# Other start addresses for the expert matmuls' operands: split weights on multiples of 128 bytes, tokens and activations 64 bytes past one

## The chip, the cores and the metric

One core of one Trainium2 chip runs the whole program. The metric is the device time in microseconds of one execution; the kernel before was run three times.

## The reference, cut to what matters

A two-layer decoder trunk for 256 tokens of width 1024, float32. Layer 0 is a recurrent mixer and a dense SwiGLU, layer 1 attention and a mixture of eight experts, of which each token takes two:

```python
h = h + rglru_mixer(rmsnorm(h), ...)
h = h + swiglu(rmsnorm(h), ffn_w_gate, ffn_w_up, ffn_w_down)       # width 3584
h = h + swa_sink_mixer(rmsnorm(h), ...)
for e in range(8):                                                   # top 2 of 8
    out += comb[..., e:e+1] * (silu(h @ w_gate[e]) * (h @ w_up[e])) @ w_down[e]
h = h + out
return rmsnorm(h)
```

The experts' weights are 8 x 3 x 1024 x 3584 floats, 352 MB, and their matmuls are most of the work.

## The kernel before, in words

**Precision.** Float32 matmuls in the experts and the dense layers are replaced by three passes in the type fp32r: each operand is split into a high part (a cast) and a low part (the operand less its high part), and the passes are high by high, low tokens by high weights, high tokens by low weights (`PASSES`, L1437).

**Weights.** SyncE loads pieces of 1 MB (128 partitions x 2048 floats) into `ring`, 14 slots. ScalarE copies a slot into `w_hi` (L663, for the experts) and VectorE writes slot less `w_hi` into `w_lo` (L1252). Both have three parts (`PARTS`), used in turn. `hi_done`, `lo_done` and `parts_used` are the counters between the three engines; a slot is loaded again when `lo_done` says that it has been split (`load`, L416 to L431). The dense layers use the same parts, through `split_dense` (L478, L841), 56 pieces in all (`SPLITS`), and the experts go on from there.

**Experts.** For one expert up to 96 tokens (`CAP`) are gathered into `xg_hi` and `xg_lo`, eight chunks of 128 x 96. The width 3584 is done in 14 steps of 256 (`NCH`). In a step, `gate_up` (L1842 to L1852) does gate and up: the stationary operand is a chunk of `xg`, the moving one 256 columns of a weight piece, 3 x 8 matmuls each. `turn_h` (L1854) transposes the product, `stage_ht` casts it to `ht_hi` and `ht_lo`, and `down` (L1861 to L1875) takes these as stationary operand and moves 512 columns of the down piece, 12 matmuls. So there are 8 x 14 = 112 steps with 48 matmuls at L1850 and 12 at L1872. `cross` overlaps an expert's end with the next one's start; `scatter` (L1819) adds an expert's output back, with `y_hi`, `y_lo` stationary and `gt_r` moving.

**Dense layers.** In `ffn_gate_up` (L1540) it is the other way round: weights are stationary (128 columns), activations `u_hi`, `u_lo` move (256 columns). `project_back` (L1486) and `project_out` (L1705) do the same with `z` and the heads. `project` (L1602) of attention has activations stationary (128 columns) and weights moving (256).

**Addresses.** Tensors lie one after the other. `ring` starts on a multiple of 128 bytes, and `gap`, 16 floats, lies behind it, so `w_hi` and `w_lo` start 64 bytes past a multiple of 128. `gap2`, 16 floats, brings what follows (`h`, `hn`, `work`, ..., `xg_hi`, `xg_lo`, `ht_hi`, `ht_lo`, `cst`) back onto multiples. The dense activations and `y_hi`, `gt_r`, `y_lo` are views laid over this memory by a first list of tensors ("below"), on multiples of 128 too. Below, "+64" is 64 bytes past a multiple of 128, and "0" is on one.

| matmul | stationary | moving |
|---|---|---|
| experts L1850, L1872 | xg, ht: 0 | w_hi, w_lo: +64 |
| dense L1540, L1486, L1705 | w_hi, w_lo: +64 | u, z, heads: 0 |
| attention L1602 | u: 0 | w_hi, w_lo: +64 |
| scatter L1819 | y: 0 | gt_r: 0 |

**Order.** Every engine's order is written out by hand. ScalarE enters the experts by `first_lead` (L704): first split, staging of xg, further splits, after `keep_tokens` (L648). TensorE's last use of a dense part is the end of `project_out(3)` (called at L1775), before the router's results.

Of the kernel before, what the change touches and what calls it, by code (L numbers as in the profile page):

```python
# [19 lines left out]
P = 128  # L20
D = 1024
KC = D // P
T = 256
# [15 lines left out]
SLOTS = 14  # L39
DENSE = 7  # L40
SLOT = 2048
PARTS = 3
PIECES = 3 * NCH

MAX_OVER = (TOPK * T - 1) // CAP
# [4 lines left out]

LRU_LOADS, FFN_LOADS, ATT_LOADS = 13, PIECES, 10
GATES_AT = 4
# [4 lines left out]
ATT_SPLITS = LRU_SPLITS + FFN_LOADS  # L57
SPLITS = ATT_SPLITS + ATT_LOADS
FIRST_SPLIT = LRU_LOADS - LRU_SPLITS
BELOW_Y = 16 + 2 * PARTS * SLOT + 16 + KC * T + D  # L60
BELOW_GT = 2048 + 4 * CAP
ORDER_MOE = [(DENSE_LOADS + n) % DENSE for n in range(DENSE)] + list(range(DENSE, SLOTS))

# [3 lines left out]
F32 = mybir.dt.float32  # L67
F32R = mybir.dt.float32r
# [51 lines left out]
def trunk(nc, x, positions, params, lru_gates, lru_w_in, lru_w_out, attn_w_qkv, attn_b_qkv, attn_sinks, attn_w_o,  # L120
          ffn_w_gate, ffn_w_up, ffn_w_down, moe_w_gate, moe_w_up, moe_w_down, norm_final, consts, out):
    with ExitStack() as ctx:
        def sb(name, shape, dt=F32):
            return ctx.enter_context(nc.sbuf_tensor(name, shape, dt))

        def sem(name):
            return ctx.enter_context(nc.semaphore(name))

        with (nc.sbuf_tensor("below", [P, 7 * SLOT], F32), nc.sbuf_tensor("z_lo", [P, KC, T], F32R) as z_lo,
              nc.sbuf_tensor("below_aa", [P, SLOT], F32), nc.sbuf_tensor("z_hi", [P, KC, T], F32R) as z_hi,  # L130
              nc.sbuf_tensor("below_u", [P, SLOT], F32), nc.sbuf_tensor("u_hi", [P, KC, T], F32R) as u_hi,
              nc.sbuf_tensor("u_lo", [P, KC, T], F32R) as u_lo, nc.sbuf_tensor("f_hi", [P, 2, 2, T], F32R) as f_hi,
              nc.sbuf_tensor("f_lo", [P, 2, 2, T], F32R) as f_lo, nc.sbuf_tensor("below_y", [P, BELOW_Y], F32),
              nc.sbuf_tensor("y_hi", [P, D], F32R) as y_hi, nc.sbuf_tensor("below_gt", [P, BELOW_GT], F32),
              nc.sbuf_tensor("gt_r", [P, T], F32R) as gt_r, nc.sbuf_tensor("y_lo", [P, D], F32R) as y_lo):
            pass
        ring = sb("ring", [P, SLOTS, SLOT])
        gap = sb("gap", [P, 16])
        w_hi, w_lo = sb("w_hi", [P, PARTS, SLOT], F32R), sb("w_lo", [P, PARTS, SLOT], F32R)
        gap2 = sb("gap2", [P, 16])  # L140
        h = sb("h", [P, KC, T])
        hn = sb("hn", [P, KC, T])
        work = sb("work", [P, 2048])
# [3 lines left out]
        zero_mem = sb("zero_mem", [1, 512], BF16)  # L147
        mask_mem = sb("mask_mem", [P, 4 * P], BF16)

        xg_hi, xg_lo = sb("xg_hi", [P, KC, CAP], F32R), sb("xg_lo", [P, KC, CAP], F32R)  # L150
        ht_hi, ht_lo = sb("ht_hi", [P, 2, 2, CAP], F32R), sb("ht_lo", [P, 2, 2, CAP], F32R)
        cst = sb("cst", [P, NCONST])
        par = sb("par", [P, NPAR])
        small = sb("small", [P, 256])
# [131 lines left out]
        hi_done, lo_done, parts_used = sem("hi_done"), sem("lo_done"), sem("parts_used")  # L286
# [19 lines left out]
        def load_of(j):  # L306
            return FIRST_SPLIT + j

        def slot_at(j):
            return slot_of[load_of(j)]  # L310
# [61 lines left out]
        def _(sp):  # L372
# [43 lines left out]
            def load(i, e, at, places, first=False):  # L416

                for n, (what, c, ahead) in enumerate(places, at):
# [5 lines left out]
                    else:  # L424
                        sp.wait_ge(lo_done, PIECES * i + (SPLITS - SLOTS + n + 1))
                    if what == "down":
# [28 lines left out]
        def _(act):  # L455
# [17 lines left out]
            def split_dense(j):  # L473

                act.wait_ge(loaded[slot_at(j)], arrive[load_of(j)])
                if j >= PARTS:
                    act.wait_ge(parts_used, j - PARTS + 1)
                nc.scalar.copy(w_hi[:, j % PARTS], ring[:, slot_at(j)]).then_inc(hi_done, 1)  # L478

# [87 lines left out]

            for j in range(PARTS, FFN_LOADS + 1):
                if j < FFN_LOADS:
                    split_dense(LRU_SPLITS + j)  # L570
                what, c = FFN_PIECES[j - PARTS] if j < FFN_LOADS else ("up", NCH - 1)
# [86 lines left out]
            def split(i, n):  # L658

                s = ORDER_MOE[n % SLOTS]  # L660
                act.wait_ge(loaded[s], 48 * i + (moe_base[s] + 16 * (n // SLOTS + 1)))
                act.wait_ge(parts_used, PIECES * i + (SPLITS - PARTS + n + 1))
                nc.scalar.copy(w_hi[:, (SPLITS + n) % PARTS], ring[:, s]).then_inc(hi_done, 1)  # L663

            def weights_back(i):
                act.wait_ge(g_turned, i + 1)
# [7 lines left out]
            def stage_xg(i):  # L674
                for g in range(2):
                    act.wait_ge(gathered, 2 * i + (g + 1))
                    nc.scalar.copy(xg_hi[:, 4 * g:4 * g + 4], ps[:, 4 + g, 0:4 * CAP].rearrange("p (c n) -> p c n", c=4)).then_inc(xg_hi_ready, 1)

            def silu(i, c, up_at):
                act.wait_ge(parts_used, PIECES * i + (SPLITS + up_at + 1))  # L680
                nc.scalar.activation(h_tok[:, c % 2], ps[0:CAP, c % 2, 0:CHF], ACT.Silu).then_inc(m_silu, 1)
# [5 lines left out]
            def stage_y(i, down_at):  # L687
                act.wait_ge(parts_used, PIECES * i + (SPLITS + down_at + 1))
                nc.scalar.copy(y_tok[:, 0:512], ps[0:CAP, 2, :]).then_inc(y_staged, 1)

            def split_y(i, down_at):
                act.wait_ge(parts_used, PIECES * i + (SPLITS + down_at + 1))
                act.wait_ge(slot_w_ready, i)
                for m in range(2):
                    nc.scalar.activation(y_hi[0:CAP, 512 * m:512 * m + 512], ps[0:CAP, 2 + m, :], ACT.Copy, scale=slot_w[0:CAP]).then_inc(y_hi_ready, 1)

            def lead(i):
                split(i, 0)
                split(i, 1)
                split(i, 2)  # L700
                split(i, 3)
                silu(i, 0, 1)

            def first_lead():  # L704
                split(0, 0)
                stage_xg(0)
                split(0, 1)
                split(0, 2)
                act.wait_ge(gap_ready, 1)
                nc.scalar.activation(gate[:, 0:2], gate[:, 0:2], ACT.Exp).then_inc(gap_exp, 1)  # L710
                split(0, 3)
                silu(0, 0, 1)
# [28 lines left out]
            def finish(i, first=False):  # L741
# [11 lines left out]
                stage_y(i, END_AT + 1)  # L753

            first_lead()
            body(0, None)
            for i in range(E - 1):
# [27 lines left out]
        def _(dve):  # L785
# [8 lines left out]
            V = nc.vector  # L794
# [7 lines left out]
            a, n = ROWS["lam"]  # L802
# [3 lines left out]
            a, n = ROWS["b_a"]  # L806
# [182 lines left out]
            for j in range(PARTS, FFN_LOADS + 1):  # L989
                what, c = FFN_PIECES[j - PARTS] if j < FFN_LOADS else ("up", NCH - 1)  # L990
# [257 lines left out]
            def split(i, n):  # L1248

                part = (SPLITS + n) % PARTS  # L1250
                dve.wait_ge(hi_done, PIECES * i + (SPLITS + n + 1))
                V.tensor_tensor(w_lo[:, part], ring[:, ORDER_MOE[n % SLOTS]], w_hi[:, part].bitcast(F32),  # L1252
                                ALU.subtract).then_inc(lo_done, 1)

            def stage_xg(i):
# [36 lines left out]
            def lead(i):  # L1292
                split(i, 0)
                split(i, 1)
                split(i, 2)
                split(i, 3)
                gate_times_up(i, 0)
# [133 lines left out]
        def _(pe):  # L1431
# [391 lines left out]
            def parts(i, n):  # L1823

                pe.wait_ge(hi_done, PIECES * i + (SPLITS + n + 1))
                return w_hi[:, (SPLITS + n) % PARTS], w_lo[:, (SPLITS + n) % PARTS]

            def low_part(i, n):

# [175 lines left out]
```

## Time and profile before

| | |
|---|---|
| median of 3 runs | 1464.48 us (1464.02 to 1464.84) |
| span of the profiled execution | 1463.9 us |
| TensorE matmul busy | 1434.9 us |
| VectorE busy | 1167.5 us |
| ScalarE busy | 925.6 us |
| read from HBM | 423.44 MB |

The profiled execution is one run by itself; its span stands 0.6 us under the median of the runs. TensorE's matmuls overlap: a row of the timeline gives the start of the first of a run of matmuls and the time to the end of the last, so the pace is read from the starts of rows that follow each other.

### The profile page before, as it was taken

To read this page: it belongs to the slowest core of one execution; us is meant where nothing else is said; L and a number is where in the kernel's file an instruction comes from. 1 tells how busy PE (TensorE), PEld (TensorE's weight loads), DVE (VectorE), ACT (ScalarE), POOL (GpSimd) and SP (SyncE) were. 2 spreads that over 40 slices of the span, in tenths; PEclk is the share of its full clock that TensorE was granted. 3 is DMA by queue.
4 is the path that set the end of the run, shared out by engine and by line. 5 is a ranking of instruction groups with operands and counts; after the bars stand their busy time and mean duration, and the time that the engine had idled before them with its cause. 6 is when DMAs were issued, how large, how long until landed. Compare 5 with 4: busy or idle time off the path is not lost.

```text
span 1463.9 us, 25480 instructions
## 1 busy us (share of the span) xinstructions
PE 1434.9 (98%) x10712; PEld 1312.7 (90%) x10712; DVE 1167.5 (80%) x1101; ACT 925.6 (63%) x918; POOL 42.5 (3%) x62
## 2 busy tenths in 40 slices
PE   7999999999999999999999999999999999999996
PEld 6899999998889889999999888999999898999994
DVE  6676556568637998998988998899798889989895
ACT  3845434444516777776776767676676767767675
POOL 2030000003020000000000000000000000000000
PEclk9999999999998999999999999999999999999998
DMA  8466555553219998999999999899999989999931
GB/s 332 144 227 227 189 189 199 199 184 136 72 49 417 368 382 336 366 363 339 357 348 368 332 378 360 335 357 353 351 349 361 367 342 354 357 350 360 355 146 45
DMA packets 60001, 426.14 MB, mean 291 GB/s; under 512 B 7025, under 2 KB 7153, under 8 KB 8689
## 3 DMA queue, kind: packets, MB, share of 16 engines
q1 hardware_dynamic: 58752, 422.60, 77.5%
q10 hardware_dynamic: 1136, 1.91, 0.4%
q8 instruction: 86, 1.41, 0.4%
q14 instruction: 27, 0.21, 0.0%
HBM read 423.44 MB, written 1.05 MB: 290 GB/s over the span
## 4 chain that ended last, share of the span: by engine, by line
PE 96%; ACT 1%; DVE 1%; POOL 1%; issue 1%; DMA 0%; ACTq 0%; SPq 0%; POOLq 0%; DVEq 0%
PE ps L1850 42%; PE ps L1872 21%; PE ps L1540 10%; PE ps L1563 5%; PE ps L1454 3%; PE ps L1838 2%; PE ps L1602 2%; PE ps L1486 2%; PE ps L1705 1%; PE ps L1857 1%; PE ps L1819 1%; PE ps L1649 1%; PE ps L1469 1%; POOL hn L1412 1%; PE ps L1677 0%
## 5 line engine op out<-in xcount | busy, mean ns | idle before, releaser
L1252 DVE TENSOR_TENSOR w_lo<-ring,w_hi 128x2048 fp32r<-128x2048 f32 x336 | 766.6, 2290 | 98.7 <-ACT w_hi L663 96.7
L663 ACT CAST w_hi<-ring 128x2048 fp32r<-128x2048 f32 x336 | 641.0, 1911 | 163.4 <-PE ps L1850 163.4
L1850 PE MATMUL ps<-w_hi,xg_hi 128*96 128x256 f32 x1792 | 248.6, 281 | 1.2 <-DVE xg_lo L1258 1.2
L1850 PE MATMUL ps<-w_hi,xg_lo 128*96 128x256 f32 x1792 | 241.8, 277 | 0.0
L1850 PE MATMUL ps<-w_lo,xg_hi 128*96 128x256 f32 x1792 | 241.6, 277 | 0.0
L1850 PEld LDWEIGHTS ps<-w_hi,xg_lo 128*96 128x96 f32 x1792 | 216.0, 161 | 0.0
L1850 PEld LDWEIGHTS ps<-w_lo,xg_hi 128*96 128x96 f32 x1792 | 215.7, 161 | 0.0
L1850 PEld LDWEIGHTS ps<-w_hi,xg_hi 128*96 128x96 f32 x1792 | 214.2, 162 | 1.3 <-DVE xg_lo L1258 1.3
L841 DVE TENSOR_TENSOR w_lo<-ring,w_hi 128x2048 fp32r<-128x2048 f32 x56 | 130.1, 2325 | 74.1 <-ACT w_hi L478 74.0
L478 ACT CAST w_hi<-ring 128x2048 fp32r<-128x2048 f32 x56 | 106.7, 1907 | 98.3 <-PE ps L1540 87.4
L1872 PE MATMUL ps<-w_lo,ht_hi 128*96 128x512 f32 x448 | 123.5, 397 | 0.2 <-DVE w_lo L1252 0.2
L1872 PE MATMUL ps<-w_hi,ht_hi 128*96 128x512 f32 x448 | 122.3, 395 | 0.3 <-ACT w_hi L663 0.3
L1872 PE MATMUL ps<-w_hi,ht_lo 128*96 128x512 f32 x448 | 122.2, 394 | 0.0
L1872 PEld LDWEIGHTS ps<-w_lo,ht_hi 128*96 128x96 f32 x448 | 72.1, 161 | 33.1 <-DVE w_lo L1252 0.7
L1872 PEld LDWEIGHTS ps<-w_hi,ht_lo 128*96 128x96 f32 x448 | 72.3, 161 | 31.7
L685 ACT CAST ht_hi<-ps 128x192 fp32r<-128x192 f32 x112 | 35.7, 319 | 91.5 <-PE ps L1857 91.2
L1872 PEld LDWEIGHTS ps<-w_hi,ht_hi 128*96 128x96 f32 x448 | 67.1, 162 | 15.9 <-ACT w_hi L663 0.5
L1540 PE MATMUL ps<-u_hi,w_hi 128*128 128x256 f32 x448 | 55.8, 277 | 0.0
L1540 PE MATMUL ps<-u_lo,w_hi 128*128 128x256 f32 x448 | 55.5, 276 | 0.0
L1540 PE MATMUL ps<-u_hi,w_lo 128*128 128x256 f32 x448 | 55.5, 276 | 0.0
L1540 PEld LDWEIGHTS ps<-u_hi,w_hi 128*128 128x128 f32 x448 | 53.0, 188 | 0.5 <-issue 0.4
L1268 DVE TENSOR_TENSOR ht_lo<-ps,ht_hi 128x192 fp32r<-128x192 f32 x112 | 38.6, 345 | 18.2 <-ACT ht_hi L685 18.2
(286 smaller groups left out, 1376.4 us busy)
## 6 DMA issues: line engine op xcount, KB each, us to landing
ring<-in_moe_w_gate SPq DMA_DIRECT2D x112, 1024.0 KB, 6.8
ring<-in_moe_w_up SPq DMA_DIRECT2D x112, 1024.0 KB, 6.7
ring<-in_moe_w_down SPq DMA_DIRECT2D x112, 1024.0 KB, 6.8
ring<-in_ffn_w_gate SPq DMA_DIRECT2D x14, 1024.0 KB, 4.8
ring<-in_ffn_w_up SPq DMA_DIRECT2D x14, 1024.0 KB, 4.8
ring<-in_ffn_w_down SPq DMA_DIRECT2D x14, 1024.0 KB, 4.9
ring<-in_lru_w_in SPq DMA_DIRECT2D x7, 1024.0 KB, 12.4
ring<-in_attn_w_qkv SPq DMA_DIRECT2D x6, 1024.0 KB, 4.8
```

The lines of the kernel that those rows point to most:

```text
L478: nc.scalar.copy(w_hi[:, j % PARTS], ring[:, slot_at(j)]).then_inc(hi_done, 1)
L663: nc.scalar.copy(w_hi[:, (SPLITS + n) % PARTS], ring[:, s]).then_inc(hi_done, 1)
L685: nc.scalar.copy(ht_hi[:, c % 2], ps[:, 6 + c % 2, 0:2 * CAP].rearrange("p (f n) -> p f n", f=2)).then_inc(ht_hi_ready, 1)
L841: V.tensor_tensor(w_lo[:, j % PARTS], ring[:, slot_at(j)], w_hi[:, j % PARTS].bitcast(F32), ALU.subtract).then_inc(lo_done, 1)
L1252: V.tensor_tensor(w_lo[:, part], ring[:, ORDER_MOE[n % SLOTS]], w_hi[:, part].bitcast(F32), ALU.subtract).then_inc(lo_done, 1)
L1268: V.tensor_tensor(ht_lo[:, c % 2], ps[:, 6 + c % 2, 0:2 * CAP].rearrange("p (f n) -> p f n", f=2), ht_hi[:, c % 2].bitcast(F32), ALU.subtr ...
L1454: mm = nc.tensor.matmul(ps[:, p % 4, f * T:(f + 1) * T], col[:, k, f * P:(f + 1) * P], u_raw[:, k], start=(k == 0), stop=(k == KC - 1))
L1486: mm = nc.tensor.matmul(ps[:, p, f * T:(f + 1) * T], w[b][:, k, f * P:(f + 1) * P], zs[a][:, k], start=False, stop=(k == KC - 1 and b == 1 ...
L1540: mm = nc.tensor.matmul(ps[:, 2 * (c % 2) + f, m * T:(m + 1) * T], w[b][:, k, f * P:(f + 1) * P], us[a][:, k], start=(j > 1 and k == 0 and ...
L1563: mm = nc.tensor.matmul(ps[:, 4 + d // 2, (d % 2) * T:(d % 2 + 1) * T], w[b][:, f, d * P:(d + 1) * P], fs[a][:, c % 2, f], start=False, st ...
L1850: mm = nc.tensor.matmul(ps[0:CAP, c % 2, m * CHF:(m + 1) * CHF], xs[a][:, k], w[b][:, k], start=(k == 0 and (a, b) == (0, 0)), stop=(k == ...
L1872: mm = nc.tensor.matmul(ps[0:CAP, 2 + g, :], hs[a][:, c % 2, f], w[b][:, f, g * 512:(g + 1) * 512], start=(c == 0 and f == 0 and (a, b) == ...
```

## The change

`w_hi` and `w_lo` each become a piece of memory with 16 floats (`SHIFT`) before and behind the three parts. The views `w_hi`, `w_lo`, used by the dense layers and attention, begin 16 floats into it and stay 64 bytes past a multiple of 128. A second pair of views, `e_hi` and `e_lo`, begins at its start, on a multiple of 128, and is what the experts' splits write and their matmuls read. The gaps move: one before `xg_hi` puts `xg` and `ht` 64 bytes past a multiple, one behind `ht_lo` brings the rest back. Since part k of the second views covers the end of part k - 1 of the first, ScalarE waits, before the experts' first split, until all 56 dense pieces have been used, where it waited for 54. The padding is counted in `BELOW_Y`.

```diff
+SHIFT = 16
-BELOW_Y = 16 + 2 * PARTS * SLOT + 16 + KC * T + D
+BELOW_Y = 2 * (SHIFT + PARTS * SLOT + SHIFT) + KC * T + D
...
         ring = sb("ring", [P, SLOTS, SLOT])
-        gap = sb("gap", [P, 16])
-        w_hi, w_lo = sb("w_hi", [P, PARTS, SLOT], F32R), sb("w_lo", [P, PARTS, SLOT], F32R)
-        gap2 = sb("gap2", [P, 16])
+        w_hi_mem = sb("w_hi", [P, SHIFT + PARTS * SLOT + SHIFT], F32R)
+        w_lo_mem = sb("w_lo", [P, SHIFT + PARTS * SLOT + SHIFT], F32R)
+        w_hi, w_lo = (a[:, SHIFT:SHIFT + PARTS * SLOT].rearrange("p (n c) -> p n c", n=PARTS) for a in (w_hi_mem, w_lo_mem))
+        e_hi, e_lo = (a[:, 0:PARTS * SLOT].rearrange("p (n c) -> p n c", n=PARTS) for a in (w_hi_mem, w_lo_mem))
...
+        gap = sb("gap", [P, SHIFT])
         xg_hi, xg_lo = sb("xg_hi", [P, KC, CAP], F32R), sb("xg_lo", [P, KC, CAP], F32R)
         ht_hi, ht_lo = sb("ht_hi", [P, 2, 2, CAP], F32R), sb("ht_lo", [P, 2, 2, CAP], F32R)
+        gap2 = sb("gap2", [P, SHIFT])
...
             def split(i, n):                       # ScalarE
...
-                nc.scalar.copy(w_hi[:, (SPLITS + n) % PARTS], ring[:, s]).then_inc(hi_done, 1)
+                nc.scalar.copy(e_hi[:, (SPLITS + n) % PARTS], ring[:, s]).then_inc(hi_done, 1)
...
             def first_lead():
+                act.wait_ge(parts_used, SPLITS)
                 split(0, 0)
...
-                V.tensor_tensor(w_lo[:, part], ring[:, ORDER_MOE[n % SLOTS]], w_hi[:, part].bitcast(F32),
+                V.tensor_tensor(e_lo[:, part], ring[:, ORDER_MOE[n % SLOTS]], e_hi[:, part].bitcast(F32),
                                 ALU.subtract).then_inc(lo_done, 1)
...
             def parts(i, n):                       # TensorE
                 pe.wait_ge(hi_done, PIECES * i + (SPLITS + n + 1))
-                return w_hi[:, (SPLITS + n) % PARTS], w_lo[:, (SPLITS + n) % PARTS]
+                return e_hi[:, (SPLITS + n) % PARTS], e_lo[:, (SPLITS + n) % PARTS]
```

## Rows read from the trace of the kernel before

**Rows 1.** The page's span, and its 40 slices: TensorE's clock, DMA share, rate.
```profile
span 1463.9 us, 25480 instructions
PE 1434.9 (98%) x10712; PEld 1312.7 (90%) x10712; DVE 1167.5 (80%) x1101; ACT 925.6 (63%) x918; POOL 42.5 (3%) x62
...
PEclk9999999999998999999999999999999999999998
DMA  8466555553219998999999999899999989999931
GB/s 332 144 227 227 189 189 199 199 184 136 72 49 417 368 382 336 366 363 339 357 348 368 332 378 360 335 357 353 351 349 361 367 342 354 357 350 360 355 146 45
```

**Rows 2.** The page's chain that ended last, shares of the span by line.
```profile
PE ps L1850 42%; PE ps L1872 21%; PE ps L1540 10%; PE ps L1563 5%; PE ps L1454 3%; PE ps L1838 2%; PE ps L1602 2%; PE ps L1486 2%; PE ps L1705 1%; PE ps L1857 1%; PE ps L1819 1%; PE ps L1649 1%; PE ps L1469 1%; POOL hn L1412 1%; PE ps L1677 0%
```

**Rows 3.** One expert: us, busy PE, PEld, DVE, ACT, POOL, clock, DMA share, GB/s.
```profile
577.00:702.00 125.00, 125.00 (x927) 112.75 (x927) 109.83 (x83) 89.26 (x76) 0.00 (x0) 1.00 0.95 354
```

**Rows 4.** Waits: who for whom, us in total, times, longest us.
```profile
ACT w_hi L663 <- PE ps L1850: 163.4, 204, 1.7
```

**Rows 5.** Timeline of TensorE, a quick step: start us, us, operation, count.
```profile
585.89 1.14 PE L1850 MATMUL ps<-w_hi,xg_hi 128*96 128x256 f32 x8
586.87 1.07 PE L1850 MATMUL ps<-w_hi,xg_lo 128*96 128x256 f32 x8
587.77 1.07 PE L1850 MATMUL ps<-w_lo,xg_hi 128*96 128x256 f32 x8
...
591.40 1.09 PE L1872 MATMUL ps<-w_hi,ht_hi 128*96 128x512 f32 x4
...
594.20 0.33 PE L1857 MATMUL ps<-cst,hn 96*128 96x96 f32 x2
```

**Rows 6.** Timeline of TensorE, a slow step.
```profile
613.29 1.10 PE L1850 MATMUL ps<-w_hi,xg_lo 128*96 128x256 f32 x8
614.23 1.10 PE L1850 MATMUL ps<-w_lo,xg_hi 128*96 128x256 f32 x8
...
617.97 1.09 PE L1872 MATMUL ps<-w_hi,ht_hi 128*96 128x512 f32 x4
...
620.76 0.33 PE L1857 MATMUL ps<-cst,hn 96*128 96x96 f32 x2
```

**Rows 7.** Timeline of TensorE in the dense feed-forward layer.
```profile
161.05 1.98 PE L1540 MATMUL ps<-u_lo,w_hi 128*128 128x256 f32 x16
...
164.68 1.52 PE L1540 MATMUL ps<-u_hi,w_hi 128*128 128x256 f32 x12
```

**Rows 8.** Timeline of TensorE: projections of attention, and a scatter.
```profile
331.27 2.04 PE L1602 MATMUL ps<-w_lo,u_hi 128*128 128x256 f32 x16
...
345.82 1.98 PE L1602 MATMUL ps<-w_lo,u_hi 128*128 128x256 f32 x16
...
435.16 2.05 PE L1705 MATMUL ps<-u_hi,w_lo 128*128 128x256 f32 x16
...
603.06 0.28 PE L1819 MATMUL ps<-gt_r,y_hi 96*128 96x256 f32 x1
...
603.65 0.28 PE L1819 MATMUL ps<-gt_r,y_lo 96*128 96x256 f32 x1
```

**Rows 9.** The page's groups: busy us, mean ns, idle before and releaser.
```profile
L1252 DVE TENSOR_TENSOR w_lo<-ring,w_hi 128x2048 fp32r<-128x2048 f32 x336 | 766.6, 2290 | 98.7 <-ACT w_hi L663 96.7
L663 ACT CAST w_hi<-ring 128x2048 fp32r<-128x2048 f32 x336 | 641.0, 1911 | 163.4 <-PE ps L1850 163.4
...
L1850 PE MATMUL ps<-w_hi,xg_lo 128*96 128x256 f32 x1792 | 241.8, 277 | 0.0
L1850 PE MATMUL ps<-w_lo,xg_hi 128*96 128x256 f32 x1792 | 241.6, 277 | 0.0
...
L1540 PE MATMUL ps<-u_hi,w_lo 128*128 128x256 f32 x448 | 55.5, 276 | 0.0
```

**Rows 10.** Timeline of ScalarE at the entry of the experts.
```profile
442.62 1.90 ACT L663 CAST w_hi<-ring 128x2048 fp32r<-128x2048 f32 x1
```

## The prediction

> **What bounds the kernel now.** I began with the page of the kernel before. TensorE is busy for 98% of the span at full granted clock, POOL hardly works, and the DMA engines are loaded in the second two thirds [rows 1]. The chain that ended last, by line, is TensorE's too: 42% of the span at L1850 (gate and up of the experts) and 21% at L1872 (down), so the two lines that the change touches hold 63% of what sets the end [rows 2]. The stretch of one expert says how much room the others have: in 125 us TensorE works for 125, VectorE for 109.83, ScalarE for 89.26, and DMA moves 354 GB/s [rows 3]. Of the waits, ScalarE's weight copies stand 163.4 us behind L1850 and show no wait for a load: data and splits are early, TensorE is late [rows 4]. So time can only be won or lost by how fast a matmul follows the one before it.
>
> That pace is not a row's mean duration, since matmuls overlap; it is the distance from start to start in the timeline. In a quick step of expert 1, eight 256-column matmuls start at 586.87 and the next eight at 587.77, and such a row is 1.07 us long [rows 5]. In a slow step of the same expert the rows are 1.10 us and 0.94 apart [rows 6]. So 113.4 ns a matmul in one and some 117 in the other: with 276 to 277 ns for the last of eight [rows 9], (1.07 - 0.276)/7 = 113.4 and (1.10 - 0.276)/7 = 117.7. Same code, same addresses, same clock. Over the whole program the 1792 matmuls of w_hi with xg_lo are busy 241.8 us, 224 rows of eight [rows 9]: 1.079 us a row, a third of the way from 1.07 to 1.10.
>
> **What the addresses have to do with it.** The change alters the address (modulo 128 bytes) of both operands of these two lines and no instruction count, so the question is which pairings the trace already shows. Before, the experts have moving +64, stationary 0. The dense feed-forward L1540 has the pairing that the change makes, stationary weights at +64 and moving activations at 0: two rows of 16 go from 161.05 to 164.68, 3.63/32 = 113.4 ns [rows 7], and over all 448 of one part 55.5 us in 28 rows is 1.98 us each [rows 9], as in [rows 7]: this pairing is at the quick pace throughout, although VectorE and ScalarE split there too. The attention projection L1602 has the pairing of before, with 128 columns: 2.04 us for 16 in one place and 1.98 in another [rows 8], slow and quick. Two rows speak against a simple rule: L1705, stationary +64 and moving 0, takes 2.05 for 16 [rows 8], so the new pairing can be slow too. And the scatter L1819, both at 0, takes (603.65 - 603.06)/5 = 118 ns [rows 8].
>
> The Trainium skill speaks against any effect: "SBUF — State Buffer" (Who interferes with whom) gives TensorE two independent read ports, for the moving operand and for LDWEIGHTS, and says that TensorE waits on nobody; its specifications count lines of 16 bytes, of which a shift of 64 is a whole number. By it the sum below would be zero. The trace has no run with one address alone changed; its two paces at one address [rows 5, 6] neither follow from the page nor refute it.
>
> **The change, term by term.** All against the profiled execution, 1463.9 us of span; the median of the runs is 1464.48, 0.6 more, and I carry differences over to it.
> - Gate and up, L1850: 5376 matmuls, 672 rows of eight. If all go at the dense pace, a row goes from 1.079 to 1.07. The part w_lo with xg_hi, at 241.6 us, gives the same; I take the first part alike beyond its entry. 672 x 0.0095 = 6.4 us gained. Bounds: nothing, or all at 1.10 and 672 x 0.021 = 14 us lost.
> - Down, L1872: 1344 matmuls of 512 columns, 112 groups of 12. Here 591.40 to 594.20 is 2.80 us, and in the slow step 617.97 to 620.76 is 2.79 [rows 5, 6]: 233 ns each, in both kinds of step. Twice the quick pace would be 226.8, that is 112 x 12 x 6.2 = 8.4 us. No row shows 512 columns of this type from a multiple of 128, so the bounds are 0 and 8.4 gained; below zero, twice 117.7 would lose 112 x 12 x 2.4 = 3.2. L1872 is nearest to L1850 in operands, and L1850 is nearer the quick end, but its own pace is not; I take the half, 4 us.
> - The entry of each step: the first eight after the transposes take 1.14 in [rows 5], 0.07 over the rest, 112 times. Shifted operands could take it away (8 us) or leave it. I leave it, and use it for the low end.
> - Second views of w_hi and w_lo, in ScalarE's copy L663 (1911 ns) and VectorE's subtraction L1252 (2290 ns) [rows 9]: written and read 64 bytes lower. Nothing shows their speed by address. A change of 5% either way is 0.1 us on a copy, 336 times beside TensorE; VectorE has 15 us free in 125 [rows 3]. Cost nothing. If VectorE took 14% more, that cover would be gone and it would set the pace.
> - Casts and subtractions that write xg and ht 64 bytes on: the same, small, hidden.
> - The new wait of ScalarE, parts_used at SPLITS (56) before the first expert copy, where 54 was asked: the last dense part is used at 435.16 + 2.05 = 437.21 [rows 8]; the copy starts at 442.62, because it stands in the queue behind others [rows 10]. It is met 5.4 us early. Queued behind it are the copy, the staging of xg and then, through VectorE, TensorE's first expert matmul; none is delayed. Cost nothing.
> - 256 bytes more per partition, with h, work and what follows on the same place modulo 128: nothing.
> - What is late next: at 10 us less, loads must come at 354 x 1.01 = 358 GB/s. In one slice of the experts they came at 417, in the two after it at 368 and 382 [rows 1]. It fits.
>
> Sum: -6.4 - 4 = -10.4, so 1463.9 becomes 1453.5, and the median 1464.5 becomes 1454.
>
> **The rivals.**
> - No effect (the rule above as a mechanism): the two paces come from something the shift leaves alone, the phase in which each run of matmuls starts after a transpose or a scatter. For it: a step switches pace without an address having changed [rows 5, 6], and the dense pairing is found slow as well [rows 8]. Against it: thousands of dense matmuls without a slow stretch [rows 7, 9]. Then 1464.5, with 2 us either way from chance.
> - Slower: the stationary tiles at +64 with 96 columns (384 bytes apart) lock into the slow pace, which L1705 shows for stationary +64 and L1850 in a third of its rows. The place is L1850, the price 672 x 0.021 = 14 us, and down adds up to 3: up to 1481. It decides for slower from about 45% of slow rows on, where now it is 32% and the range of no change ends.
> - DMA takes over: the loads are at a busy share of 0.95 in the experts [rows 3]. If 358 GB/s can't be had, the gain stops near 1460. I give this little.
> - Larger gain: all of down and the entries as well, -6.4 - 8.4 - 8 = 1441.7. Also little.
>
> **How the numbers follow.** Forecast of a gain in either size 0.6, in that 0.05 for the larger and 0.05 for the stopped one; no effect 0.23; slower 0.17. About 0.2%, 2.9 us, is what a measurement of this kernel can tell from no change. The likeliest case by itself reaches from 1449.7 (both lines in full) to 1461. For 8 in 10 I take in no effect and the smaller part of the slower case, up to 1470, and below go to 1445, for a part of the entries. Most of the slower case and the rest of the larger gain are left out.
>
> **What would show it.** Right: rows of eight at L1850 at 1.07 in every step, the group of w_hi with xg_lo near 239.7 us, L1872's groups of 12 under 2.80, LDWEIGHTS as before, ScalarE and VectorE idle no more than a little less, granted clock 1.00. Wrong: 1.10 in a third of the steps as now (no effect), or in more of them (slower); 2.80 left in down takes 4 us from the sum. If TensorE shows idle time behind L1252 or L663 in the experts, the cover of the splits was gone and my terms for them failed; if ScalarE's copy at 442.6 moved, the wait was not free.

## The result, and the profile after

The changed kernel takes 1473.6 us (1473.44 to 1474.05, four runs), the kernel before 1464.66 in the same comparison: ratio 1.0063, 95% interval 1.0049 to 1.0078. It is slower by 9 us, where 1454 was forecast, and lies above the 1470 that the range allowed. A run's time stands 1.8 to 2.0 us over its own span in every kernel of this study, so spans of profiled executions can be compared with each other: 1463.9 before [rows 1], 1471.5 after, 7.6 more.

The page of the changed kernel: its span, what answers to [rows 2], the clock line, and the groups that answer to [rows 9] (L1857 is the old L1850, L1879 the old L1872).

```profile
span 1471.5 us, 25480 instructions
...
PEclk9999999999999999999999999999999999999998
...
PE ps L1857 43%; PE ps L1879 21%; PE ps L1547 10%; PE ps L1570 5%; PE ps L1461 3%; PE ps L1845 2%; PE ps L1609 2%; PE ps L1493 2%; PE ps L1712 1%; PE ps L1864 1%; PE ps L1826 1%; PE ps L1656 1%; PE ps L1476 1%; POOL hn L1419 1%; PE ps L1684 0%
...
L1259 DVE TENSOR_TENSOR w_lo<-ring,w_hi 128x2048 fp32r<-128x2048 f32 x336 | 767.1, 2291 | 106.6 <-ACT w_hi L669 105.3
L669 ACT CAST w_hi<-ring 128x2048 fp32r<-128x2048 f32 x336 | 642.8, 1916 | 172.4 <-PE ps L1857 172.3
L1857 PE MATMUL ps<-w_hi,xg_hi 128*96 128x256 f32 x1792 | 250.4, 282 | 1.2 <-DVE xg_lo L1265 1.2
L1857 PE MATMUL ps<-w_lo,xg_hi 128*96 128x256 f32 x1792 | 248.8, 281 | 0.0
L1857 PE MATMUL ps<-w_hi,xg_lo 128*96 128x256 f32 x1792 | 243.5, 278 | 0.0
...
L1547 PE MATMUL ps<-u_hi,w_lo 128*128 128x256 f32 x448 | 55.5, 276 | 0.0
```

The copies and subtractions take what they took (1911 to 1916 ns, 2290 to 2291), ScalarE waits longer for TensorE than before, and the dense layers stand at 55.5 us. The loss sits in one group above all: w_lo with xg_hi, 241.6 to 248.8 us; w_hi with xg_lo grew by 1.7. Where in a step this happens, the timeline of TensorE shows for the step that answers to [rows 5]: start us, us, operation, count.

```profile
585.89 1.14 PE L1857 MATMUL ps<-w_hi,xg_hi 128*96 128x256 f32 x8
586.87 1.07 PE L1857 MATMUL ps<-w_hi,xg_lo 128*96 128x256 f32 x8
587.78 1.11 PE L1857 MATMUL ps<-w_lo,xg_hi 128*96 128x256 f32 x8
588.73 1.10 PE L1857 MATMUL ps<-w_hi,xg_hi 128*96 128x256 f32 x8
589.66 1.10 PE L1857 MATMUL ps<-w_hi,xg_lo 128*96 128x256 f32 x8
590.60 1.11 PE L1857 MATMUL ps<-w_lo,xg_hi 128*96 128x256 f32 x8
591.54 1.10 PE L1879 MATMUL ps<-w_hi,ht_hi 128*96 128x512 f32 x4
...
594.32 0.33 PE L1864 MATMUL ps<-cst,hn 96*128 96x96 f32 x2
```

The step begins quick, as before (1.14, 1.07). At the first row that moves w_lo it goes to 1.11, and it stays slow through the up projection. Before, a step was quick or slow as a whole [rows 5, 6]. The down matmuls gained: 591.54 to 594.32 is 2.78 us for 12, where it was 2.80.

The starts in the traces give the price. From the first start of a pass (eight matmuls) to the first of the next a quick pass takes 907 ns and a slow one 933; in the change the pass in which w_lo follows w_hi takes 953, and 947 where the pace was slow already. Of the 112 steps 73 were quick before. In the change 80 enter quick, and all 80 lose it at w_lo; their gate and up take 5.649 us, where a quick step took 5.511. That is 80 x 0.138 = 11.0 us. Slow steps went from 5.651 to 5.678, and there are 32 where there were 39; with that the sum for gate and up is 10.9 us, 622.7 to 633.6. Down, 1.9 us less, and small differences elsewhere make it 7.6 in the span.

That pointed to w_lo's place relative to w_hi. Before, they lay 24576 bytes apart, a multiple of 256. The padding makes it 24704, a multiple of 128 only, so `e_hi` stands at 128 and `e_lo` at 0 modulo 256. It also puts `h`, `hn`, `work` and what follows up to `xg_mem`, and `y_hi`, `gt_r`, `y_lo`, 128 bytes further modulo 256, so matmuls ahead of a step have other operands too.

### The profile page after: what moved, and what is told of

It is laid out like the page before. It is cut to its first block, busy times and chain, and to the rows that moved or that the text cites. A ratio compares the mean times of both kernels' runs of the same rounds, so it can differ in the third digit from the quotient of the medians.

```text
span 1471.5 us, 25480 instructions
## 1 busy us (share of the span) xinstructions
PE 1442.6 (98%) x10712; PEld 1321.7 (90%) x10712; DVE 1168.8 (79%) x1101; ACT 927.2 (63%) x918; POOL 42.5 (3%) x62
## 4 chain that ended last, share of the span: by engine, by line
PE 96%; ACT 1%; DVE 1%; POOL 1%; issue 1%; DMA 0%; ACTq 0%; SPq 0%; POOLq 0%; DVEq 0%
PE ps L1857 43%; PE ps L1879 21%; PE ps L1547 10%; PE ps L1570 5%; PE ps L1461 3%; PE ps L1845 2%; PE ps L1609 2%; PE ps L1493 2%; PE ps L1712 1%; PE ps L1864 1%; PE ps L1826 1%; PE ps L1656 1%; PE ps L1476 1%; POOL hn L1419 1%; PE ps L1684 0%
## 5 line engine op out<-in xcount | busy, mean ns | idle before, releaser
L1259 DVE TENSOR_TENSOR w_lo<-ring,w_hi 128x2048 fp32r<-128x2048 f32 x336 | 767.1, 2291 | 106.6 <-ACT w_hi L669 105.3
L669 ACT CAST w_hi<-ring 128x2048 fp32r<-128x2048 f32 x336 | 642.8, 1916 | 172.4 <-PE ps L1857 172.3
L1857 PE MATMUL ps<-w_hi,xg_hi 128*96 128x256 f32 x1792 | 250.4, 282 | 1.2 <-DVE xg_lo L1265 1.2
L1857 PE MATMUL ps<-w_lo,xg_hi 128*96 128x256 f32 x1792 | 248.8, 281 | 0.0
L1857 PE MATMUL ps<-w_hi,xg_lo 128*96 128x256 f32 x1792 | 243.5, 278 | 0.0
L1857 PEld LDWEIGHTS ps<-w_lo,xg_hi 128*96 128x96 f32 x1792 | 221.7, 162 | 0.0
L1857 PEld LDWEIGHTS ps<-w_hi,xg_lo 128*96 128x96 f32 x1792 | 217.4, 161 | 0.0
L1857 PEld LDWEIGHTS ps<-w_hi,xg_hi 128*96 128x96 f32 x1792 | 216.2, 162 | 1.3 <-DVE xg_lo L1265 1.3
L1879 PE MATMUL ps<-w_hi,ht_hi 128*96 128x512 f32 x448 | 123.8, 398 | 0.3 <-ACT w_hi L669 0.3
L1879 PE MATMUL ps<-w_hi,ht_lo 128*96 128x512 f32 x448 | 121.4, 392 | 0.0
L1879 PE MATMUL ps<-w_lo,ht_hi 128*96 128x512 f32 x448 | 120.9, 392 | 0.2 <-DVE w_lo L1259 0.2
L1879 PEld LDWEIGHTS ps<-w_hi,ht_lo 128*96 128x96 f32 x448 | 72.2, 161 | 32.1
L1879 PEld LDWEIGHTS ps<-w_lo,ht_hi 128*96 128x96 f32 x448 | 72.0, 161 | 31.1 <-DVE w_lo L1259 0.7
L1879 PEld LDWEIGHTS ps<-w_hi,ht_hi 128*96 128x96 f32 x448 | 67.1, 161 | 17.3 <-ACT w_hi L669 0.5
L1547 PE MATMUL ps<-u_hi,w_hi 128*128 128x256 f32 x448 | 55.8, 277 | 0.0
L1547 PE MATMUL ps<-u_hi,w_lo 128*128 128x256 f32 x448 | 55.5, 276 | 0.0
L1547 PE MATMUL ps<-u_lo,w_hi 128*128 128x256 f32 x448 | 55.5, 276 | 0.0
L1547 PEld LDWEIGHTS ps<-u_lo,w_hi 128*128 128x128 f32 x448 | 52.9, 188 | 0.0
## 6 DMA issues: line engine op xcount, KB each, us to landing
ring<-in_lru_w_in SPq DMA_DIRECT2D x7, 1024.0 KB, 12.5
```

The lines of the kernel that those rows point to most:

```text
L669: nc.scalar.copy(e_hi[:, (SPLITS + n) % PARTS], ring[:, s]).then_inc(hi_done, 1)
L1259: V.tensor_tensor(e_lo[:, part], ring[:, ORDER_MOE[n % SLOTS]], e_hi[:, part].bitcast(F32), ALU.subtract).then_inc(lo_done, 1)
L1547: mm = nc.tensor.matmul(ps[:, 2 * (c % 2) + f, m * T:(m + 1) * T], w[b][:, k, f * P:(f + 1) * P], us[a][:, k], start=(j > 1 and k == 0 and ...
L1857: mm = nc.tensor.matmul(ps[0:CAP, c % 2, m * CHF:(m + 1) * CHF], xs[a][:, k], w[b][:, k], start=(k == 0 and (a, b) == (0, 0)), stop=(k == ...
L1879: mm = nc.tensor.matmul(ps[0:CAP, 2 + g, :], hs[a][:, c % 2, f], w[b][:, f, g * 512:(g + 1) * 512], start=(c == 0 and f == 0 and (a, b) == ...
```

## The experiments

I tell places modulo 256 from here on. "Quick passes" counts the 672 passes of eight at L1850 whose matmuls follow each other, from the fourth on, at under 115 ns on the average; it is worked out from the starts in each trace. With both operands on one place modulo 128 some passes come near that limit (in e3 165 stand at 115.0 ns and one at 114.75, in e4 59 at 115.0), but from its first start to the next pass's each of them takes 929 ns or more, as slow ones do. All times are medians beside the kernel before on the same chip (1464.0 to 1464.8 there), with the ratio's 95% interval.

| kernel | moving hi / lo | xg | time, us | interval of the ratio | quick passes |
|---|---|---|---|---|---|
| before | 192 / 192 | 0 | 1464.66 | | 438 |
| the change | 128 / 0 | 192 | 1473.6 | 1.0049 to 1.0078 | 160 |
| e1 | 128 / 128 | 64 | 1462.79 | 0.9980 to 0.9998 | 498 |
| e2 | 192 / 64 | 128 | 1475.52 | 1.0060 to 1.0088 | 87 |
| e3 | 128 / 0 | 128 | 1475.84 | 1.0064 to 1.0092 | 1 |
| e4 | 192 / 64 | 192 | 1475.61 | 1.0064 to 1.0092 | 0 |
| e5 | 192 / 192 | 128 | 1471.98 | 1.0038 to 1.0065 | 486 |
| e6 | 128 / 128 | 192 | 1472.61 | 1.0040 to 1.0067 | 144 |
| e7 | 128 / 128 | 0 | 1475.93 | 1.0060 to 1.0088 | 0 |
| e8 | 128 / 128 | 64, ht 128 | 1469.98 | 1.0026 to 1.0054 | 180 |
| e9 | 128 / 128 | 64 | 1459.92 | 0.9956 to 0.9980 | 576 |
| e10 | 128 / 0 | 192, xg_lo 64 | 1471.64 | 1.0029 to 1.0060 | 292 |
| e11 | 128 / 128 | 64 | 1462.12 | 0.9974 to 0.9992 | 528 |
| e12 | 128 / 128 | 64 | 1458.62 | 0.9950 to 0.9977 | 629 |

`ht` and `cst` moved as well: where the table has no word of `ht`, it stands with `xg`. `cst` stands at 0 before, in the change, e3, e4, e6 and e10, at 128 in e1, e2, e5, e7, e8 and e9, at 192 in e11 and e12. `hn` stands at 128 in the change, e2, e3, e4, e5 and e10, at 0 in the others.

### First four: the distance between w_hi and w_lo, and each shift by itself

e1, on the changed kernel, puts w_lo back on w_hi's place:

```diff
-BELOW_Y = 2 * (SHIFT + PARTS * SLOT + SHIFT) + KC * T + D
+BELOW_Y = 2 * (SHIFT + PARTS * SLOT + SHIFT) + KC * T + D + 32
+        gap3 = sb("gap3", [P, 32])                    # between w_hi_mem and w_lo_mem
```

> The changed kernel with 128 bytes more between the memory of w_hi and that of w_lo. In the changed kernel e_hi and e_lo stand at different places modulo 256 (before, w_hi and w_lo stood at the same one); here they stand at the same one again. Theory 'distance' (the slow pace at the first w_lo matmul comes from the 128 bytes of padding between the two pieces): the w_lo with xg_hi group falls from 248.8 us towards 242, total about 1464. Theory 'pair' (moving at 0 with stationary at +64 is itself the slower pairing for 96 columns): nothing changes, 1473 to 1474.

e2, on the kernel before, has the same 32 floats between `w_hi` and `w_lo` and in `BELOW_Y`, and nothing else.

> The kernel before with 128 bytes between w_hi and w_lo, nothing else. Theory 'distance': it becomes slow like the changed kernel, about 1473, with the w_lo with xg_hi group near 249 us. Theory 'pair': as before, 1464.5.

e3 is the changed kernel with `gap` moved behind `ht_lo`, so that only the moving operands are shifted:

```diff
-        gap = sb("gap", [P, SHIFT])                   # before xg_hi
-        gap2 = sb("gap2", [P, SHIFT])                 # behind ht_lo
+        gap = sb("gap", [P, 2 * SHIFT])               # behind ht_lo
```

> The changed kernel with xg and ht on multiples of 128 as before: only the moving operands are shifted (moving 0, stationary 0, as in the scatter, whose matmuls follow at 118 ns). Theory 'pair': at least as slow as the changed kernel in gate and up, 1474 to 1480 (every row of eight at 1.10 or more). Theory 'distance': slow only in the w_lo passes, 1473.

e4 is the changed kernel with the second views on the place of the first, so that only the stationary operands are shifted:

```diff
-        e_hi, e_lo = (a[:, 0:PARTS * SLOT].rearrange(...) for a in (w_hi_mem, w_lo_mem))
+        e_hi, e_lo = (a[:, SHIFT:SHIFT + PARTS * SLOT].rearrange(...) for a in (w_hi_mem, w_lo_mem))
```

> The changed kernel with the second views at +64 like the first: only the stationary operands are shifted (moving +64, stationary +64). Theory 'pair': the same place modulo 128 for both, slow as in the run with both on 0, 1474 to 1480. Theory 'distance': 1473, since the padding is there.

e1 gives back all of the loss, 1462.79, and e2 makes the kernel before as slow as the change and slower, 1475.52, by 10.8 and 10.9 us. Both went as the theory of the distance had them, with one miss: e2's w_lo group was to be near 249 us and is 245.2, while w_hi with xg_hi rose from 248.6 to 253.2. But neither moves w_lo alone. The 32 floats push everything behind w_lo 128 bytes further too, `xg`, `ht` and `cst` with it, and the next four runs show that this counts. So 10.8 us is not the price of the distance by itself, nor are the 1.9 us of e1 under the kernel before the worth of the shift that the title names; for both there are cleaner runs below, e2 against e5 and e6 against the kernel before. A quick step of e1, from the timeline of TensorE: the passes hold their pace into w_lo.

```profile
594.05 1.07 PE L1858 MATMUL ps<-w_hi,xg_hi 128*96 128x256 f32 x8
594.96 1.07 PE L1858 MATMUL ps<-w_hi,xg_lo 128*96 128x256 f32 x8
595.86 1.07 PE L1858 MATMUL ps<-w_lo,xg_hi 128*96 128x256 f32 x8
596.77 1.07 PE L1880 MATMUL ps<-w_hi,ht_hi 128*96 128x512 f32 x4
```

In e2 the place where the pace is lost is another one: the step that begins quick loses it where w_hi follows w_lo, not where w_lo follows w_hi. It is so in all 29 steps that begin quick there.

```profile
606.75 1.07 PE L1852 MATMUL ps<-w_hi,xg_lo 128*96 128x256 f32 x8
607.66 1.09 PE L1852 MATMUL ps<-w_lo,xg_hi 128*96 128x256 f32 x8
608.58 1.11 PE L1852 MATMUL ps<-w_hi,xg_hi 128*96 128x256 f32 x8
609.53 1.09 PE L1852 MATMUL ps<-w_hi,xg_lo 128*96 128x256 f32 x8
```

In e3 and e4 both operands stand on the same place modulo 128, where before and in the change they are 64 bytes apart; no step is quick, and both times lie in the range of 1474 to 1480 expected for that. The two have other addresses and the same distance between moving and stationary, and their page groups agree to 0.1 us in the down matmuls, though in gate and up they differ by up to 0.9 us (w_hi with xg_lo, 245.9 and 246.8). First e3, then e4.

```profile
L1878 PE MATMUL ps<-w_hi,ht_hi 128*96 128x512 f32 x448 | 120.8, 391 | 0.3 <-ACT w_hi L668 0.3
```

```profile
L1879 PE MATMUL ps<-w_hi,ht_hi 128*96 128x512 f32 x448 | 120.8, 391 | 0.3 <-ACT w_hi L669 0.3
```

### Second four: is it the distance between moving and stationary?

e5 is the kernel before with `gap2` at 48 floats instead of 16 (and `BELOW_Y` with it).

> The kernel before with everything behind w_lo 128 bytes further: moving operands stay at +64, xg and ht stay on multiples of 128, only their distance to the weights moves from 192 to 64 modulo 256, the distance of the run with the changed kernel and 128 bytes more. Theory 'distance' (what counts is moving less stationary, and w_hi and w_lo alike): 1462.8, down groups hi by hi near 228.8 ns a matmul. Theory 'multiples of 128 for the moving operand': nothing changes, 1464.6.

e6, e7 and e8 are e1 with, in turn, `gap` (before `xg_hi`) at 48 floats instead of 16; `gap` moved behind `ht_lo`, as in e3; `gap2` moved to between `xg_lo` and `ht_hi`.

> The changed kernel with 128 bytes more between w_hi and w_lo, and xg and ht 128 bytes further: places modulo 128 as in the changed kernel, distances modulo 256 as in the kernel before (192). Theory 'distance': the pace of the kernel before, 1464.6, down hi by hi near 232.7 ns. Theory 'multiples of 128': as in the run with the 128 bytes alone, 1462.8.

> The changed kernel with 128 bytes more between w_hi and w_lo, xg and ht on multiples of 128: both operands at 0, and w_hi and w_lo alike. If only the padding between w_hi and w_lo does the harm: about 1464. If a distance of 0 between moving and stationary modulo 128 is slow by itself: gate and up at 117 ns or more with uneven rows, 1470 or more.

> The changed kernel with 128 bytes more between w_hi and w_lo, xg at +64 as there and ht alone on a multiple of 128. In the two runs with distance 0 modulo 128 the down matmuls were the quickest (229.3, 232.2, 231.4 ns). Theory 'distance': gate and up as in the run with the 128 bytes alone, down 1344 x 1.7 ns = 2.3 us less, 1460.5. If the down matmuls were quick for the 128 bytes between w_hi and w_lo and not for this: 1463.

Of the four expectations only e7's held: both operands on one place modulo 128 is slow by itself, 1475.93 and no quick pass, with w_hi and w_lo alike. e5 missed by 9 us, e6 by 8, e8 by 9.5. Their traces say why.

e5 did in the experts what was expected: the page shows the groups of e1 to 0.2 us, though both operands' addresses differ by 64. First e5, then e1.

```profile
L1850 PE MATMUL ps<-w_hi,xg_lo 128*96 128x256 f32 x1792 | 241.2, 277 | 0.0
L1850 PE MATMUL ps<-w_lo,xg_hi 128*96 128x256 f32 x1792 | 241.2, 277 | 0.0
L1872 PE MATMUL ps<-w_hi,ht_hi 128*96 128x512 f32 x448 | 120.7, 391 | 0.3 <-ACT w_hi L663 0.3
```

```profile
L1858 PE MATMUL ps<-w_hi,xg_lo 128*96 128x256 f32 x1792 | 241.2, 277 | 0.0
L1858 PE MATMUL ps<-w_lo,xg_hi 128*96 128x256 f32 x1792 | 241.0, 277 | 0.0
L1880 PE MATMUL ps<-w_hi,ht_hi 128*96 128x512 f32 x448 | 120.6, 391 | 0.3 <-ACT w_hi L670 0.3
```

The time went in the dense feed-forward layer, where no operand had moved: L1540 takes 57.8, 57.4 and 57.4 us where it took 55.8, 55.5 and 55.5, and L1563 29.8 three times where it took 28.8, some 9 us together. The timeline of e5 shows where that began.

```profile
97.46 1.07 PE L1486 MATMUL ps<-z_hi,w_lo 128*128 128x256 f32 x8
...
104.56 0.59 PE L1448 MATMUL ps<-hn,cst 128*128 128x256 f32 x2
104.80 2.24 PE L1540 MATMUL ps<-u_hi,w_hi 128*128 128x256 f32 x16
106.87 2.05 PE L1540 MATMUL ps<-u_lo,w_hi 128*128 128x256 f32 x16
...
163.40 2.05 PE L1540 MATMUL ps<-u_lo,w_hi 128*128 128x256 f32 x16
```

The matmul of L1448 has `cst` and a part of `hn` as operands, both 128 bytes further in e5. After it the dense matmuls run at 2.05 for 16, and they still do at 163 us, where [rows 7] had 1.98. So a pace persists: matmuls keep what they had, over two hundred microseconds, until something ends it. With `hn` alone 128 bytes further (the change) or `cst` alone (e1) the dense layer stays quick.

e2 has the same two operands on the same places, and the same slow pace behind that matmul, but there it ends. In e2 the stationary w_lo stands 128 bytes from w_hi, and the pace comes back where w_hi follows the first w_lo: the distances are 1.88 us for 16, then 1.84, then 1.81 (115.51 less 113.70).

```profile
105.79 0.59 PE L1450 MATMUL ps<-hn,cst 128*128 128x256 f32 x2
...
109.98 2.04 PE L1542 MATMUL ps<-u_hi,w_lo 128*128 128x256 f32 x16
111.86 1.99 PE L1542 MATMUL ps<-u_hi,w_hi 128*128 128x256 f32 x16
113.70 1.98 PE L1542 MATMUL ps<-u_lo,w_hi 128*128 128x256 f32 x16
115.51 1.98 PE L1542 MATMUL ps<-u_hi,w_lo 128*128 128x256 f32 x16
```

Modulo 256, e2 and e5 differ in w_lo's place and in nothing else, so this pair shows what the 128 bytes between w_hi and w_lo do. By the starts in the traces they cost 12.5 us in gate and up (634.2 against 621.7) and save 8.5 in the dense feed-forward layer (229.1 against 237.6); the times are 1475.52 and 1471.98.

e6 is the cleanest run of the title's change. In it `hn`, `cst`, `gt_r` and all else stand modulo 256 where they stand in the kernel before, w_hi and w_lo are alike, and only w_hi, w_lo, `xg` and `ht` are 64 bytes lower. It takes 1472.61 us, 7.9 more than the kernel before beside it: the shift alone is slower. By the starts gate and up take 630.7 us, 8.0 more, and down 314.8, as before; 24 of the 112 steps are quick where 73 were. The groups of e6:

```profile
L1858 PE MATMUL ps<-w_hi,xg_hi 128*96 128x256 f32 x1792 | 251.1, 282 | 1.2 <-DVE xg_lo L1266 1.2
L1858 PE MATMUL ps<-w_hi,xg_lo 128*96 128x256 f32 x1792 | 244.7, 278 | 0.0
L1858 PE MATMUL ps<-w_lo,xg_hi 128*96 128x256 f32 x1792 | 244.3, 278 | 0.0
```

It speaks against the theory of the distance too, since moving and stationary stand as far apart modulo 256 as in the kernel before, 192 bytes. The changed kernel, which has w_lo on another place and what lies from `h` to `xg_mem` 128 bytes further, is only 1.0 us slower than e6: more of its steps enter quick, 80, and all lose it at w_lo.

e6 and e8 are the same in the experts: within a step all six passes have one pace, and steps are slow that were quick, because a step enters slow. e8 moves only `ht`, and gate and up, whose operands did not move, rose from 241.2 to 243.9 us in w_hi with xg_lo.

### Third three: what sets the pace of a step

Each line below is one expert, each group one step, each letter one pass of eight (q quick, s slow); Y marks the scatters. It is worked out from the starts in the traces, and is the same for experts 2 to 7; the first has no scatter in it, and behind the last comes no gather.

```
before  qqqqqq qqqqqq qqqqqq Y ssssss ssssss Y ssssss qqqqqq ssssss ssssss qqqqqq qqqqqq qqqqqq qqqqqq qqqqqq
change  qqssss qqssss qqssss Y ssssss qqssss Y ssssss qqssss qqssss qqssss qqssss qqssss ssssss ssssss qqssss
e1      ssssss qqqqqq qqqqqq Y ssssss qqqqqq Y ssssss qqqqqq qqqqqq qqqqqq qqqqqq qqqqqq ssssss qqqqqq qqqqqq
e9      ssssss qqqqqq qqqqqq Y qqqqqq qqqqqq Y qqqqqq qqqqqq qqqqqq qqqqqq qqqqqq qqqqqq ssssss qqqqqq qqqqqq
e10     qqssqs qqssqs qqssqs Y ssssqs qqssqs Y ssssqs qqssqs qqssqs qqssqs qqssqs qqssqs sqssqs sqssqs qqssqs
```

e1 has four slow steps: the first, the two behind scatters, and the one behind the gather of the next expert. e9 shifts the scatter's moving operand, on e1:

```diff
-BELOW_GT = 2048 + 4 * CAP
+BELOW_GT = 2048 + 4 * CAP + SHIFT
+              nc.sbuf_tensor("below_lo", [P, SHIFT], F32),   # between gt_r and y_lo
+        gap4 = sb("gap4", [P, SHIFT])                         # before gt_mem
+        gap5 = sb("gap5", [P, SHIFT])                         # behind gt_mem
-        gap = sb("gap", [P, SHIFT])
+        gap = sb("gap", [P, SHIFT + 32])
```

> The changed kernel with 128 bytes more between w_hi and w_lo, and gt_r, the scatter's moving operand, on +64 instead of 0 (its stationary y_hi and y_lo stay on multiples of 128). Theory 'lock' (a run of matmuls keeps the pace it enters with; matmuls with both operands at 0 leave it slow): the scatters follow at 113 to 114 ns instead of 118 to 120, and the two steps behind scatters in each expert become quick, 16 steps x 0.17 = 2.7 us less than the 1462.8 of the run without it, 1460. Theory that the entry has nothing to do with it: 1462.8.

It held to 0.1 us: 1459.92. The count behind it was a little off: 14 steps behind scatters turned quick and not 16, and in expert 1 one step net went the other way, 78 passes more in all. To move `gt_r`, e9 also puts `y_lo`, `xg_mem` and `mask_mem` 128 bytes further, so it does not show by itself that `gt_r` alone did it. The timeline shows the scatters at (602.40 - 601.84)/5 = 112 ns, where [rows 8] had 118, and the step behind them quick from its first pass on.

```profile
601.84 0.28 PE L1830 MATMUL ps<-gt_r,y_hi 96*128 96x256 f32 x1
...
602.40 0.28 PE L1830 MATMUL ps<-gt_r,y_lo 96*128 96x256 f32 x1
602.52 1.09 PE L1861 MATMUL ps<-w_hi,xg_hi 128*96 128x256 f32 x8
603.45 1.07 PE L1861 MATMUL ps<-w_hi,xg_lo 128*96 128x256 f32 x8
```

The same scatter in e1 has the step behind it at 1.11:

```profile
618.55 0.28 PE L1827 MATMUL ps<-gt_r,y_lo 96*128 96x256 f32 x1
618.68 1.11 PE L1858 MATMUL ps<-w_hi,xg_hi 128*96 128x256 f32 x8
```

e10, on the changed kernel, moves the other operand's jump:

```diff
+        gap4 = sb("gap4", [P, 32])                    # between xg_hi and xg_lo
+        gap5 = sb("gap5", [P, 32])                    # behind xg_lo
```

> The changed kernel with 128 bytes more between xg_hi and xg_lo (ht stays where it is modulo 256). In the changed kernel the quick pace is lost where the passes go from w_hi to w_lo, the third pass of a step. Theory 'lock' (a jump of 128 bytes modulo 256 in moving less stationary ends the quick pace): it is now lost one pass earlier, where the stationary operand jumps, so the w_hi with xg_lo group grows by about a quarter to half of what the third pass shows, to 246 to 249 us, and the time is 1475 to 1476. Theory that reading w_lo is what is slow, wherever it stands: 1473.6 and that group unchanged at 243.5.

The jump of the stationary operand did not end the quick pace, it brought it back: the second pass is quick in all 112 steps in up and in 98 in gate (not in the 14 behind scatters), even where the first was slow, and the group w_hi with xg_lo fell to 240.2 us instead of growing. The time, 1471.64, is 2 us under the change and not 2 over, so neither theory of e10 held. The timeline of e10:

```profile
596.16 1.07 PE L1860 MATMUL ps<-w_hi,xg_lo 128*96 128x256 f32 x8
597.06 1.11 PE L1860 MATMUL ps<-w_lo,xg_hi 128*96 128x256 f32 x8
598.02 1.10 PE L1860 MATMUL ps<-w_hi,xg_hi 128*96 128x256 f32 x8
598.95 1.07 PE L1860 MATMUL ps<-w_hi,xg_lo 128*96 128x256 f32 x8
599.86 1.11 PE L1860 MATMUL ps<-w_lo,xg_hi 128*96 128x256 f32 x8
```

So the rival of e10, that reading w_lo is what is slow, fell already with e1 and e2, and my own form of "lock" had the direction wrong. What stands is narrower: a pace changes at a jump of 128 bytes in one of the operands, or at an entry; some jumps end the quick pace (w_hi to w_lo in the change, w_lo to w_hi in e2), others restore it (w_lo to w_hi in the dense layer of e2, xg_hi to xg_lo in e10). In the eight kernels with w_hi and w_lo alike, `xg_hi` and `xg_lo` alike and 64 bytes modulo 128 between moving and stationary, a step keeps one pace in all its six passes, in every one of the 112 but for a single pass of e12 that stands at the limit.

e11 is e1 with `gap2`, ahead of `cst`, at 32 floats.

> The changed kernel with 128 bytes more between w_hi and w_lo, and cst (whose identity is the moving operand of the two transposes ahead of each step) 64 bytes further; no operand of gate and up or down moves. Theory 'lock': which steps are quick changes with it, so the time moves by more than 1 us either way from 1462.8, and within a step all passes keep one pace. Theory that a step's pace depends on its own operands alone: 1462.8, the same steps quick.

1462.12 against 1462.79 is not a move of more than 1 us, so by its number this missed. The traces agree with the theory all the same: the first step of experts 2 to 8 turned from slow to quick, 42 passes, the first two steps of expert 1 from quick to slow, 12 passes (498 to 528 quick ones in all), and nothing else changed, though no operand of gate and up had moved.

### Last: the two gains together

e12 is e9 with `gap2` at 32 floats.

> The two gains of the last runs together: 128 bytes more between w_hi and w_lo, gt_r on +64, cst 64 bytes further. Theory 'lock': cst decides the first step of an expert and gt_r the two behind scatters, which are different steps, so the gains add: 576 quick passes of the 672 become about 606, 30 x 0.028 = 0.8 us less than 1459.9, 1459.1. If they do not add, the entries depend on more than the matmuls just ahead of them, and it stays at 1460 or rises.

1458.62 us, ratio to the kernel before 0.9963 (0.9950 to 0.9977), with 629 quick passes, where 1459.1 and about 606 were expected. It beats both kernels: 5.4 us under the one before, 15 under the change. Of its 43 slow passes 42 are the step behind the gather in seven experts, and one stands at 115.0 ns, the limit. Against e9 alone its medians differ by 1.3 us, which is about the spread of their runs; the trace has 53 passes more. That is more than the 30 expected, since in expert 1, where e11 had lost two steps, two were gained.

## Why the prediction was wrong

- **Bottleneck: right.** TensorE's distance from start to start sets the time; the splits stayed covered, DMA followed, and the granted clock stood at nine tenths or more of full speed in all slices but the last (before, one slice in the middle stood at eight).
- **Gate and up, "if all go at the dense pace": this is the step that failed.** 6.4 us less were booked. The shift by itself, e6, put 8.0 us on: it left 24 steps quick where 73 were. I read the dense pace as the pace of the pairing, but with one and the same pairing modulo 128 a step is quick or slow as it is entered (before, e1, e6, e9, e11). The shift moves a step's operands against those of the transposes and scatters ahead of it; that this is what makes more steps enter slow in e6 is likely by e9 and e11, but no run shows it for e6. Before and after, the two operands stand 64 bytes apart modulo 128, so the change had no other distance to offer there. The dense layer entered quick and kept the pace; e5 made it slow without moving an operand of it. "Thousands of dense matmuls without a slow stretch" counted one entry many times.
- **"256 bytes more per partition, with h, work and what follows on the same place modulo 128: nothing." This failed too.** I followed addresses modulo 128 only and never compared `w_lo` with `w_hi`. In the changed kernel the loss has this form: the L1857 groups took 10.7 us more (1.8 + 1.7 + 7.2 over [rows 9] and the 248.6 us of the first pass before, shown below), and by the starts 11.0 come from the 80 steps that enter quick and lose the pace at w_lo. e2 against e5 shows on the kernel before that these 128 bytes do that, 12.5 us in gate and up. They come on top of the shift only in part: without them, in e6, most of the steps enter slow anyway, and the time is 1.0 us less.

```profile
L1850 PE MATMUL ps<-w_hi,xg_hi 128*96 128x256 f32 x1792 | 248.6, 281 | 1.2 <-DVE xg_lo L1258 1.2
```

- **Down: right in sign, half in size, and by luck.** 123.5 us and two groups of 122.3 and 122.2 before are 368.0; 123.8, 121.4 and 120.9 after are 366.1, so 1.9 us gained where 4 was booked. The shift by itself gained nothing there: e6 has 123.2, 122.7 and 122.1, again 368.0.
- **ScalarE's new wait: free, as said.** The first expert copy starts at 441.74, 0.9 us before [rows 10]:

```profile
441.74 1.90 ACT L669 CAST w_hi<-ring 128x2048 fp32r<-128x2048 f32 x1
```

- **The rivals.** The slower case had the place, L1850, and nearly the size, 10.7 us of 14, but the wrong reason: e1, e9, e11 and e12 have stationary tiles of 96 columns on +64 too and are the quickest kernels here, while e6 with them is slow. The mechanism of the no-effect case, the phase at the entry of a run, was the better reading of [rows 5, 6] and is what e9 and e11 speak for; its conclusion, that addresses would then not matter, does not follow, since addresses set the entry.
- **The Trainium skill's rule** of two independent read ports ("SBUF — State Buffer", Who interferes with whom) would have given no effect, and so would its lines of 16 bytes. The runs differ: 128 bytes in w_lo's place alone moved gate and up by 12.5 us (e2, e5), and both operands on one place modulo 128 left one pass of 2016 under the limit (e3, e4, e7). Whether ports, lines or something else is behind it no run shows. The measurement decides on the effect, not on the cause.

What stays open: why a jump ends the pace in one case and brings it back in another, what the changed kernel would take with w_lo alone moved (no run does that on it), what it is in e6 that makes so many steps enter slow, what in the gather leaves the next step slow, and how much of e6's and e8's loss each kind of entry carries. I did not try other distances than multiples of 64 bytes, nor moving `sel` or `work`.

## What to carry to other kernels

When TensorE is the bound and matmuls are a hundred nanoseconds long, read the distance from start to start pass by pass, and ask where a pace changes before asking what its mean is. Padding for one operand moves all that lies behind it: keep high and low parts on one place modulo 256 and not only 128, keep moving and stationary operands off the same place modulo 128, and list every matmul pair again after any change of layout. This is no guarantee: e6 keeps both and is slow, by its entries. A run that puts a gap in front of one tensor moves all tensors behind it, so write down every place before you put a price on one. A stretch that is quick in one layout is no proof for its pairing; look at what runs just ahead of it, and change that.

## What the runs showed that was not expected

- Two paces of the same 256-column matmul, 113.4 and about 117 ns, persist: after the matmuls of L1448 the dense layer kept the slow one for over 200 us (e5), and lost it within 8 us where w_lo stood 128 bytes from w_hi (e2).
- Equal distances between moving and stationary gave equal group times at other addresses in e5 and e1 (gate, up and down, within 0.2 us in 120 to 240) and in e3 and e4 for down alone; they did not in e6 and the kernel before, 251.1 and 248.6 us in w_hi with xg_hi.
- All four operands of gate, up and down 64 bytes lower, and nothing else moved modulo 256, cost 7.9 us (e6 against the kernel before): 24 quick steps instead of 73.
- With both operands on the same place modulo 128 no step of gate and up reached the quick pace (e3, e4, e7).
- The same 128 bytes between w_hi and w_lo cost 12.5 us where w_hi and w_lo move and saved 8.5 where they are stationary (e2 against e5).
- With moving and stationary 64 bytes apart, the scatter's matmuls of 256 columns follow at 112 ns instead of 118 (e9).
